# The second block's context keys and values: four portions of 256 columns, one in each of the last four expert pairs

## The reference, cut to what matters

```python
# first block, last layer: 16 experts, 64 tokens each
aff = softmax(h @ w_router)
gate, idx = top_k(aff.transpose(0, 2, 1), 64)
xe = h[idx]
a = silu(einsum('becd,edf->becf', xe, w_gate)) * einsum('becd,edf->becf', xe, w_up)
ye = einsum('becf,efd->becd', a, w_down) * gate[..., None]
y = zeros.at[idx].add(ye)
# second block, first step: projections of the latents and of the context
hc = modulate(ctx, g_mix, csh1, csc1)                 # 256 x 1024
p = h @ w_in                                          # for latents and for the context
q, k, v, o, gates = split(p, [512, 512, 1024, 1024, 16])
```

## Time and profile before

| | us |
|---|---|
| median of 3 runs | 1437.09 (1436.69 to 1439.11) |
| the profiled execution | 1439.5 |
| its span, first to last instruction | 1437.7 |
| expert pairs on PE (first and last matmul of line 896) | 329.8 to 796.0 |
| PE busy in the span | 1389.8 (97%) |
| DMA, mean over the span | 219 GB/s |

### The profile page before, as it was taken

How to read it: one execution, slowest core, us unless ns; L and a number is a source line. 1 busy time by engine, 2 the same in 40 slices (tenths; PEclk the granted TensorE clock), 3 DMA queues, 4 the chain that set the end, 5 groups by cost and what they waited for, 6 DMA issues and landing times.

```text
span 1437.7 us, 16626 instructions
## 1 busy us (share of the span) xinstructions
PE 1389.8 (97%) x6717; PEld 916.5 (64%) x6717; DVE 618.7 (43%) x1134; ACT 481.2 (33%) x877; POOL 94.3 (7%) x103
## 2 busy tenths in 40 slices
PE   7989999999999999998999899999999999999998
PEld 5865466864443443533443678787798888888876
DVE  5357787581122123122212653226764442443425
ACT  7355397341101102111111632435535332132323
POOL 2000000100000000000000300132011110001100
PEclk9999999999999999999999999999999999999999
DMA  7489120779999999899999423230332231331301
GB/s 244 50 327 415 69 117 3 268 298 404 424 428 426 426 429 419 359 426 424 413 386 422 135 83 102 72 112 6 107 114 80 97 117 60 116 117 59 117 30 59
DMA packets 71821, 314.92 MB, mean 219 GB/s; under 512 B 6252, under 2 KB 34701, under 8 KB 53442
## 3 DMA queue, kind: packets, MB, share of 16 engines
q1 hardware_dynamic: 69568, 309.79, 54.4%
q10 hardware_dynamic: 1346, 2.41, 1.4%
q0 software_dynamic: 832, 1.67, 0.4%
HBM read 307.55 MB, written 5.78 MB: 218 GB/s over the span
## 4 chain that ended last, share of the span: by engine, by line
PE 85%; DVE 5%; DMA 5%; ACT 3%; issue 1%; SPq 0%; POOL 0%; ACTq 0%; DVEq 0%; POOLq 0%
PE ps L896 21%; PE ps L475 14%; PE ps L476 14%; PE ps L477 14%; PE ps L846 2%; DMA sb<-in_w_up 2%; PE ps L881 2%; DMA sb<-in_w_gate 1%; PE ps L615 1%; PE ps L1183 1%; DMA sb<-in_w_down 1%; PE ps L621 1%; PE ps L759 1%; PE ps L571 1%; PE ps L882 1%
## 5 line engine op out<-in xcount | busy, mean ns | idle before, releaser
L896 PE MATMUL ps<-sb 128*64 128x512 f32 x1536 | 349.7, 602 | 8.6 <-DMA sb<-in_w_gate 3.8
L896 PEld LDWEIGHTS ps<-sb 128*64 128x64 f32 x1536 | 106.0, 137 | 208.0 <-issue 194.1
L1322 ACT ACTIVATE sb<-ps 128x512 f32<-128x512 f32 (+4 forms) x140 | 72.7, 546 | 167.2 <-PE ps L869 63.4
L476 PE MATMUL ps<-r_fl,r_top 128*128 128x512 f32 x320 | 125.7, 393 | 0.0
L477 PE MATMUL ps<-r_mid,r_low 128*128 128x512 f32 x320 | 125.4, 392 | 0.0
L475 PE MATMUL ps<-r_mid,r_top 128*128 128x512 f32 x320 | 124.9, 390 | 0.0
L2669 DVE TENSOR_TENSOR r_low<-raw,r_top 128x2048 fp32r<-128x2048 f32 x33 | 74.2, 2288 | 78.5 <-ACT r_top L1322 78.5
L2346 DVE TENSOR_TENSOR sb<-sb,ps 128x512 f32<-128x512 f32 x64 | 43.6, 686 | 133.4 <-PE ps L882 133.3
L1322 ACT ACTIVATE r_top<-raw 128x2048 fp32r<-128x2048 f32 x33 | 61.3, 1903 | 69.7 <-PE ps L477 69.7
L1652 ACT ACTIVATE sb<-ps 128x512 f32<-128x512 f32 x16 | 9.5, 596 | 198.8 <-PE ps L869 160.5
L475 PEld LDWEIGHTS ps<-r_mid,r_top 128*128 128x128 f32 x320 | 60.1, 188 | 13.6
(11 more groups left out here) (458 smaller groups left out, 2504.9 us busy)
## 6 DMA issues: line engine op xcount, KB each, us to landing
sb<-in_w_gate SPq DMA_DIRECT2D x28, 2048.0 KB, 16.8
sb<-in_w_down SPq DMA_DIRECT2D x22, 2048.0 KB, 17.1
sb<-in_w_up SPq DMA_DIRECT2D x16, 2048.0 KB, 17.1
sb<-in_w_up SPq DMA_DIRECT2D x32, 1024.0 KB, 15.9
sb<-in_w_mod SPq DMA_DIRECT2D x16, 1536.0 KB, 12.5
raw<-in_f_w_up SPq DMA_DIRECT2D x22, 1024.0 KB, 6.8
sb<-in_w_down SPq DMA_DIRECT2D x19, 1024.0 KB, 10.7
raw<-in_a_w_in SPq DMA_DIRECT2D x12, 1024.0 KB, 5.3
```

The costliest lines, as they stand in the source:

```text
L476: pe.matmul(o, a_hi, b_lo, start=False, stop=False)
L896: mm = pe.matmul(PS[64 * hf:64 * hf + 64, b * HALF:(b + 1) * HALF], lhsT(k), ring[ring_slot(c)][:, kk, hf * HALF:(hf + 1) * HALF], start=( ...
L1322: return act_(o, i_, ACT.Identity, bias=bias, scale=scale)
```

## The change

A portion becomes 256 columns over all 1024 rows: keys 0 to 255, keys 256 to 511, values 512 to 767, values 768 to 1023. One portion is computed in each of pairs 4, 5, 6 and 7, always behind group 1. The load of portion 0 stays after `hc_x`. Those of portions 1, 2 and 3 stand behind chunks 118, 142 and 166 (with 119, 143 and 167), which are the last load of the pair before. A portion is complete in one product, so each has its own sum in PSUM and ACT copies two halves of 256 columns after each. The bytes are the same; the rows that a load takes from w_in are 1 KB long where they were 2 KB.

```diff
-        CX_PAIR = {4: 0, 6: 1}
+        CX_FROM = 4
@@ PE
             def context_product(p):
-                kind, part = divmod(p, 2)
-                if part == 0:
-                    for tt in range(NCT):
-                        claim(6 + tt, ("cxe", (kind, tt)))
+                for tt in range(NCT):
+                    claim(6 + tt, ("cxe", (p, tt)))
...
                 for tt in range(NCT):
-                    for k in range(4):
-                        o = (4 * part + k) * CTXN + tt * P
-                        mm = split_product(bank(6 + tt), hc_hi[:, o:o + P], hc_lo[:, o:o + P], w_h[:, k, :], w_l[:, k, :],
-                                           part == 0 and k == 0, part == 1 and k == 3)
+                    for k in range(KD):
+                        o = k * CTXN + tt * P
+                        mm = split_product(bank(6 + tt, 256), hc_hi[:, o:o + P], hc_lo[:, o:o + P], w_h[:, k, :], w_l[:, k, :],
+                                           k == 0, k == KD - 1)
...
-                if i in CX_PAIR:
-                    context_product(2 * CX_PAIR[i])
+                if i >= CX_FROM:
+                    context_product(i - CX_FROM)
                 weights(i, 2, claim(2, ("x_sil", (i, 1))), tokens(1), adds=4)
-                if i in CX_PAIR:
-                    context_product(2 * CX_PAIR[i] + 1)
@@ ACT
-                if i in CX_PAIR:
-                    context_round(2 * CX_PAIR[i])
+                if i >= CX_FROM:
+                    context_round(i - CX_FROM)
...
-                    if i in CX_PAIR and e == 0:
-                        context_round(2 * CX_PAIR[i] + 1)
...
+                        eng.wait_ge(*at("pe_cx", p))
+                        if p < 2:
+                            a = copy(krc_first[:, tt, 256 * p:256 * p + 256], bank(6 + tt, 256), scale=MDK ** -0.5)
+                        else:
+                            a = copy(vm[:, tt, p, 0:MDV], bank(6 + tt, 256))
@@ SP
             def context_load(p):
-                kind, part = divmod(p, 2)
-                lo = 1536 if kind else 512
-                sp.dma_start(view(cx_raw[part][:, :], 4), aw[:, 4 * part:4 * part + 4, lo:lo + HALF])...
+                lo = (512, 768, 1536, 1792)[p]
+                sp.dma_start(view(cx_raw[p % 2][:, :], KD), aw[:, :, lo:lo + 256])...
...
-                if c == 102:
-                    context_load(1)
-                if c == 144:
-                    sp.wait_ge(*at("pe_cx", 0))
-                    context_load(2)
-                if c == 150:
-                    sp.wait_ge(*at("pe_cx", 1))
-                    context_load(3)
+                if c % 24 == 22 and c // 24 in (4, 5, 6):
+                    p = c // 24 - 3
+                    if p >= 2:
+                        sp.wait_ge(*at("pe_cx", p - 2))
+                    context_load(p)
```

More of the change, by code:

```diff
@@ L911, in context_product @@
                 pe.wait_ge(*at("cx_wl", p))
-                w_h, w_l = view(cx_hi[part][:, :], 4), view(cx_lo[part][:, :], 4)
+                w_h, w_l = view(cx_hi[p % 2][:, :], KD), view(cx_lo[p % 2][:, :], KD)
                 for tt in range(NCT):
-                    for k in range(4):
-                        o = (4 * part + k) * CTXN + tt * P
-                        mm = split_product(bank(6 + tt), hc_hi[:, o:o + P], hc_lo[:, o:o + P], w_h[:, k, :], w_l[:, k, :],
-                                           part == 0 and k == 0, part == 1 and k == 3)
+                    for k in range(KD):
+                        o = k * CTXN + tt * P
+                        mm = split_product(bank(6 + tt, 256), hc_hi[:, o:o + P], hc_lo[:, o:o + P], w_h[:, k, :], w_l[:, k, :],
+                                           k == 0, k == KD - 1)
                 mm.then_inc(*inc("pe_cx", p))
@@ L1639, in _ @@
             for i in range(PAIRS):
-                if i == 4:
+                if i == CX_FROM:
                     eng.wait_ge(*at("hc_in"))
                     copy(hc_hi[:, :], hc_x[:, :]).then_inc(*inc("cx_hh"))
-                if i in CX_PAIR:
-                    context_round(2 * CX_PAIR[i])
+                if i >= CX_FROM:
+                    context_round(i - CX_FROM)
                 if i == PAIRS - 1:
@@ L1652, in _ @@
                     act_(sil, bank(2 * e), ACT.Silu).then_inc(*inc("x_sil", (i, e)))
-                    if i in CX_PAIR and e == 0:
-                        context_round(2 * CX_PAIR[i] + 1)
                 eng.wait_ge(*at("x_pe_aT", (i, 0)))
                 copy(actT[0], bank(3).rearrange("p (k q) -> p k q", k=4)).then_inc(*inc("x_aT", (i, 0)))
-                if i == 4:
+                if i >= CX_FROM:
+                    p = i - CX_FROM
                     for tt in range(NCT):
[L1659 to L1664, removed]
+                        eng.wait_ge(*at("pe_cx", p))
[3 more added lines that the diff above has]
+                            a = copy(vm[:, tt, p, 0:MDV], bank(6 + tt, 256))
+                        a.then_inc(*inc("cxe", (p, tt)))
                 if i == PAIRS - 1:
@@ L2357, in _ @@
             for i in range(PAIRS):
-                if i == 4:
+                if i == CX_FROM:
                     eng.wait_ge(*at("cx_hh"))
                     ve.tensor_tensor(hc_lo[:, :], hc_x[:, :], hc_hi[:, :].bitcast(F32), ALU.subtract).then_inc(*inc("cx_hl"))
-                if i in CX_PAIR:
-                    context_rest(2 * CX_PAIR[i])
+                if i >= CX_FROM:
+                    context_rest(i - CX_FROM)
                 for n in range(4):
@@ L2366, in _ @@
                 act_rows(i, 0)
-                if i in CX_PAIR:
-                    context_rest(2 * CX_PAIR[i] + 1)
                 if i == PAIRS - 1:
@@ L2946, in context_load @@
             def context_load(p):
-                kind, part = divmod(p, 2)
-                lo = 1536 if kind else 512
-                sp.dma_start(view(cx_raw[part][:, :], 4), aw[:, 4 * part:4 * part + 4, lo:lo + HALF]).then_inc(*inc(f"cx_in{part}", p, 16))
+                lo = (512, 768, 1536, 1792)[p]
+                sp.dma_start(view(cx_raw[p % 2][:, :], KD), aw[:, :, lo:lo + 256]).then_inc(*inc(f"cx_in{p % 2}", p, 16))
             for c in range(RINGN, NCHUNK, 2):
```

## The result

The changed kernel takes 1440.74 us (median of 12 runs, 1435.15 to 1444.01). The kernel before takes 1437.95 us (12 runs, 1435.88 to 1439.29). The ratio is 1.0019, 95% interval 1.0010 to 1.0027. The change costs 2.8 us, and the forecast of 1433.7 is missed by 7.0 us, to the wrong side. The profiled execution took 1440.64 us, its span 1438.8.

What follows compares the result with a forecast made beforehand. The expert stage was taken as bound by PE and DMA in turn. By DMA, 791.3 plus 0.9 lost ends the experts at 792.2, 3.8 us sooner; 3.4 off the 1437.09 median gives 1433.7 us, range 1430.8 to 1437.6.

Steps and rivals of the forecast that it cites:

- part 3: Expert stage, new places of loads and products: lost DMA time nearly goes, 11.2 us before, 0.9 left after.
- my 792.2: Forecast end of the experts in us: 791.3 by the DMA sum plus 0.9 lost, against 795.97 before.
- The step from the profile to the median: Whole kernel: of 3.8 us won against the profiled run, 3.4 taken off the median of 1437.09, giving 1433.7.
- 48 matmuls: Context products on PE: 48 of 256 columns for 24 of 512, +0.29 us each, +1.15 for four, bounds 0 and +1.5.
- 1 KB rows: Context loads: 3.0 us per MB for 2.67 with 2 KB rows, +1.4 us of DMA in all, bounds +0 and +2.2.
- The first wait and its clock: Pair 4, wait for chunk 102: stays with its clock fall and grows by 0.3 us.
- The cover: Pairs 4 to 7: splits, scatter steps, SP's waits and ACT's copies have time to spare and cost nothing; cover 3 us.
- my 51.6: Pair 7: time in us from the landing of the chunk PE then needs to the experts' end, last product included.
- The signs: Right: long wait gone, pairs 61 to 62 us at 415 GB/s. Wrong: DMA share under 0.95, experts' end after 795.
- A: Rival, expert pairs: DMA queue stays as leaky, 3 to 5 us lost, gain 0 to 1.7, about 1436.2; chance 25%.
- B: Rival, expert pairs: ring drains at every product, 2.5 us idle each, long waits with clock falls, +5, 1442; chance 10%.

Runs made afterwards that it cites:

- e3: Changed kernel with the products of pairs 5 to 7 behind group 0 instead of group 1; 1436.93 us against 1437.56 for the kernel before.
- e9: Changed kernel with the loads of portions 1 to 3 behind chunks 110, 134 and 158; 1437.36 us against 1438.03 for the kernel before.
- e10: Changed kernel with each expert load from chunk 104 on issued one chunk later, like a ring of seven; 1452.62 us against 1438.03 for the kernel before.
- e12: Kernel before, unchanged, run once more for a second profile; 1435.25 us, span 1433.4.
- e6: Kernel before with 48 matmuls of 256 columns a product, loads untouched, context keys and values wrong; 1439.83 us against 1437.62.
- e7: Kernel before with context loads of 256 columns in 1 KB rows, products untouched, keys and values wrong; 1438.87 us against 1437.62.
- e2: Changed kernel with context loads in 8 KB rows of expert weights, keys and values wrong; 1437.61 us against 1437.56 for the kernel before.
- e1: Kernel before with the new 256-column portions at the old places of loads and products; 1440.74 us against 1437.56.
- e5: Changed kernel's places with the old portions (512 columns, half the rows, 24 matmuls); 1436.23 us against 1437.62 for the kernel before.
- e8: Changed kernel's places with old 512-column portions, products of pairs 5 to 7 moved behind group 0; 1432.81 us against 1437.62 for the kernel before.

## Why the prediction was wrong

**The step that failed** is in part 3: "Neither has the 10.9 us block that emptied the DMA queue, so the lost DMA time should nearly go", with 0.9 us left. By rows: 745.83 (chunk 172, PE starts on its landing) - 550.23 (hc_x, the row below) - 12.0 - 176.8 = 6.8 us. That is 5.9 more than I left. hc_x was 0.7 earlier than before, so chunk 172 came 5.2 us after my 740.6, and the experts' end, 797.19, is 5.0 after my 792.2.

```profile
550.23 1.91 ACT L1318 ACTIVATE r_hch<-r_hcx 128x2048 fp32r<-128x2048 f32 x1 [4.28 <-DMA r_hcx<-ctx_cols_dram]
553.22 1.91 ACT L1318 ACTIVATE r_cxh<-r_cxw 128x2048 fp32r<-128x2048 f32 x1 [1.08 <-DMA r_cxw<-in_a_w_in]
```

What misled me is that I looked for idle queue in windows of 10 and 16 us and at pairs as sums. "In the worst stretches their share is 0.86 to 0.90" is a misreading that follows from it: from 587 to 593 the share is 0.50 and 0.42, at 210 and 82 GB/s. The page shows it too, as one slice at 8 tenths and 359 GB/s (575 to 611), where I had put all slices of the expert pairs at 90% or more. A pair with one product costs PE 61.0 and DMA 61.9, and I took such near balance for no loss. But within a pair they differ by 6 to 7 us each way: in groups 1 and 2 with the product PE takes 25.9 us and DMA needs 19.6, in the rest PE takes 35.0 and DMA needs 42.3 with the context's load. Here that lost time in both directions, with a ring of eight. e3 and e9 show it by moving one thing each at equal sums (3.4 and 3.5 us), e10 by taking one slot of lead (11.8 us).

**The step from the profile to the median** failed too, for 2.0 us. I kept 3.4 of the 3.8 us as the gain on the median, as if the profiled run of before were about as good as any. It was 1.6 us above that kernel's median of 12 (1439.5 against 1437.95), and e12 shows what such a run can have more: one clock fall and a later start of the experts. The median then known, 1437.09 from 3 runs, was itself 0.9 us under that of 12. The changed kernel's profiled run lies at its median, within 0.1. 4.9 us by the profile (1440.64 against 1435.7), 2.0 by this step, and 0.1 make the 7.0.

**48 matmuls: right in the trace.** The step is (634.17 - 628.53)/47 = 0.120 us for 0.119, and e6 has +0.30 a product for +0.29. On the time it may be more than the +1.15: e6 measures +2.2, and the interval (1.0 to 3.7) reaches down to it. Whether a longer product also costs queue time stays open. The Trainium skill's fixed cost of 2.5 ns a matmul (TensorE: Matmul & The Clock Gate, "Wait — 56ns, not 53.3ns?") does not agree: 2 x 120 - 227 is 13 ns for each one added.

```profile
628.53 0.28 PE L475 MATMUL ps<-r_cxh,r_hch 128*128 128x256 f32 x1
...
634.17 0.28 PE L477 MATMUL ps<-r_cxh,r_hcl 128*128 128x256 f32 x1
```

**1 KB rows: right.** 3.0 us was said; by the two rows above portion 0 is 2.99 behind hc_x. e7 gives +1.25 us for the +1.4 of the account. The Trainium skill (DMA: Bandwidth & Descriptors, "Specifications") has transfers from 512 bytes on at line rate; with 8 KB rows at 2.47 (e2), 2 KB at 2.67 and 1 KB at 2.99 these runs do not agree.

**The first wait and its clock: right.** It grew from 1.94 to 2.47, more than the 0.3 said, and the clock behind it stayed low (0.59 over 3.5 us). Whether it falls differs from one execution to the next, as e12 shows, which I had only guessed for the spread of runs.

**The cover: right.** ACT rounds portion 1 at 610.96 without a wait for its landing, no scatter step is held, SP's waits for old products hold nothing, and from chunk 172 to the end it is 51.4 us for my 51.6. Nothing of the miss comes from there.

**The signs.** The long wait is gone and the clock there is 1.00, as said. Waits under 1.5 us: four of five, the last is 1.71. Pairs of 61 to 62 us at 415 GB/s or more: not so, from chunk 124 to 148 it is 64.1 us, from there to 172 63.3, at 410 to 414. The end after 795 was named as what would prove me wrong, and did. A DMA share under 0.95 was a useless sign: it is 1.00 in each pair, as short rows keep the engines busy at fewer bytes and a few us at 0.85 to 0.92 drown in 60.

**The rivals.** In size A was nearest by the profile: 3 to 5 us lost and an end up to 796, for 6.8 and 797.2. By the median B was, 1442, but it owes that to the 2.0 us above. In mechanism B was half right: the queue does run low at every product (the dips at 575, 650 and 710), not in plain pairs as A had it. B took 2.5 us for each; by the landings it is 3.0, 2.4 and 0.9 in pairs 4 to 6. The total stays under the 7.5 from which B was to decide, the waits of pairs 5 to 7 stay at 1.0 to 1.7, and no clock fall comes with them. My argument against B was that the queue "still had work" after the first product of pair 4; in the changed kernel its share is 0.85 at that place (575 to 578). In the kernel before it is 1.01 there, and the reason was in my own list of what changes: the load behind chunk 103 stood in the queue. With it 5.6 us of loads were left at 575.19, without it 4.2 at 575.02. And the queue fell idle from 587 on, not from 596.

**The change in two.** The places gain 1.4 us, the shapes cost 3.2 to 3.45 (e1, or e6 and e7), which makes about +2 where +2.8 (1.4 to 3.9) was measured. So spreading the work over four pairs did help. But I gave it 6.0 us (3.4 won in spite of 1.15 and 1.4 for the shape), and it brought 1.4.

## What to carry to other kernels

When two resources are both near full, compare them over the ring's depth, not over a loop iteration: list how fast the consumer draws in each part, and put foreign work of the consumer into the part that draws fastest and foreign loads into the part that draws slowest. A dip of the queue is to be looked for in windows as short as one load (3 us here) and in GB/s; longer windows and the share hide it. Before a forecast of 3 us is put on a median, take a second profile or ask what the first one's extra waits and clock falls were worth.

## What the runs showed of the hardware

- One wait, two clocks. The wait near 558 has the granted clock at 0.55 and 0.59 behind it in the first profiles of before (1.94 us) and of the changed kernel (2.47), and at 1.00 in e12 (2.34) and in e1 (2.80). In 12 profiles with this wait (1.56 to 3.09 us) the clock falls in eight, also behind the 1.86 of e2, and stays in e1, e5, e8 and e12; its length does not tell which. A fall to 1.2 GHz over 3.5 us costs 1.7 us (24 matmuls in 7.0 instead of 5.3).
- The spread of a kernel's runs is in part this. In the 12 runs of the changed kernel the mean granted clock goes from 0.993 (1444.01 us) to 0.998 (1435.15 us); the correlation with the time is -0.82, about 1.2 us for each 0.001. That falls of the clock cause all of it is not shown: late landings give waits as well.
- Load time of 1 MB on a full queue by row length: 2.99 us at 1 KB (2.86 to 2.99 in the changed kernel), 2.67 at 2 KB, 2.47 at 8 KB.
- One slot of 1 MB in a ring of eight was worth 11.8 us over 88 chunks when draw and supply differ within a pair; 5.7 us of product moved by four chunks was worth 3.4.
